# A Trainium2 kernel of two hybrid blocks: scores, pick and dense gates of the expert stage in one stage, and the expert loop's first up sums on another engine

## Chip, cores and metric

The kernel runs on one core of one Trainium2 chip. The metric is device microseconds from start to end of one execution, lower is better. TensorE, VectorE, ScalarE, GpSimd and SyncE are called PE, DVE, ACT, POOL and SP, as in the profile.

## What is computed

Two blocks follow one another on 512 tokens of width 1024. The first is a pool mixer and a gated delta rule, merged, and then an expert layer. The change lies in that layer; the second block (a state-space scan and an attention) is not touched. The expert layer, cut to what matters:

```python
q = (x @ w_query).astype(f32).reshape(b, s, PEER_HEADS, 2, PEER_HALF)       # 8 heads, 2 halves of 128
s1 = jnp.einsum("bshc,hkc->bshk", q[..., 0, :], keys_1.astype(f32))         # 128 keys a half
s2 = jnp.einsum("bshc,hkc->bshk", q[..., 1, :], keys_2.astype(f32))
v1, i1 = lax.top_k(s1, PEER_TOPK)                                           # 16 of 128
v2, i2 = lax.top_k(s2, PEER_TOPK)
cand_score = (v1[..., :, None] + v2[..., None, :]).reshape(...)
cand_idx = (i1[..., :, None] * N_KEYS + i2[..., None, :]).reshape(...)
top_score, pos = lax.top_k(cand_score, PEER_TOPK)                           # 16 of 256 pairs
experts = jnp.take_along_axis(cand_idx, pos, axis=-1)
gates = jax.nn.softmax(top_score, axis=-1)
# for each token, over its 8 x 16 experts e of 16384:
act = gelu(x . expert_down[e])
y += (gate_e * act) * expert_up[e]
```

## The kernel before, in words

Weights are streamed from HBM as tiles of 128 x 1024 fp32 (512 KB), four raw buffers deep. Each tile is split into a high part (ACT, `split_high`, L188) and a low part (DVE or POOL, `split_low`, L197), and a product is three fp32r matmuls of 512 columns (high by high, high by low, low by high), eight chunks to a tile (`mm_columns`, L212 to L214). A tile's split waits until the tile two before it is used up; the next raw load waits for both parts.

The experts are not gathered. The kernel makes a dense gate matrix for all 16384 experts: for each token a 128 x 128 matrix (first key by second key), stored in HBM as `gates`. All expert rows then go through PE: for each first key, a down tile gives 128 experts by 512 tokens, gelu and gate are applied, and an up tile is multiplied.

The stages are functions run one after another by `g.run`, each a block of five engine programs that ends in a barrier of all engines:

- `peer_scores` (L1582): 16 query tiles. PE makes a query tile (24 matmuls) and its scores against the keys (L1618), ACT copies both out, DVE picks 16 of 128 for each of 4 token tiles (`top16`, L1558: MAX8, MATCH_REPLACE8, FIND_INDEX8), POOL splits the weights' low parts and copies values and key numbers to `vals` and `keyno` (L1653).
- `peer_pick` (L1674): PE makes the first 24 down tiles (`EARLY`), ACT applies gelu into `early` (L1736), POOL splits the lows. DVE, for each of four tiles of 128 tokens: 80 candidates (L1780 to L1786), 16 of 80 by `top16`, ranks (L1796 to L1814), then the key numbers by one-hot products over 2048 elements: compare (L1817), multiply (L1822), sum (L1826), each twice; then the softmax's sum (L1829 to L1833), with the exponential on ACT (L1740). PE transposes three rows of 128 (L1751) and DVE copies them into `first`, `second`, `gate` (`keep`, L1772).
- `peer_gates` (L1843): 128 quads of 4 tokens. For each quad DVE makes four one-hot rows of the first key times the gate (L1891) and one of the second key (L1895), POOL two of the second key (L1880), ACT one in two steps (L1919, L1925); PE multiplies them (L1910); ACT copies the result into a staging buffer (L1943) and SP stores a buffer of 8 quads to HBM (L1953). The hot buffers are a ring of four quads. This stage has no down tiles; it is written as loops with register addresses.
- `peer_early` (L1984): loads the gates of 4 first keys at a time (L2005), weighs `early` with them, and multiplies the 24 up tiles.
- `peer_experts` (L2114): a loop of 25 rounds. A round makes 4 down tiles, and the up product of 4 tiles in the Strassen-Winograd form, which needs sums of up tiles. The sums of the first pair (`up_sums`, L2172 to L2177) are made by POOL for the next round, those of the second pair by DVE. ACT rounds the sums up to `up_high` (L2337), DVE makes the low part (L2466). DVE adds the products x = 0 to 6 out of PSUM (L2508).

In `peer_experts` POOL's part, and DVE's order around it, are:

```python
# POOL, L2629 to L2638
first_pair(0)
with steps(pool, 0, LOOPS, 1) as q:
    first_pair(q + 1)
# DVE, end of a round
for x in range(2, 5):
    add(q, x)
low_t43(q + 1, 0)
for x in range(5, 7):
    add(q, x)
```

## Time and profile before

| | |
|---|---|
| median of 3 runs | 3190.7 us (3184.8 to 3194.28) |
| the profiled execution | 3189.76 us, its span 3188.0 us |
| PE busy | 2984.3 us (94%) |
| DVE busy | 2114.2 us (66%) |
| ACT busy | 1287.1 us (40%) |
| POOL busy | 666.3 us (21%) |
| DMA | 312.56 MB, 98 GB/s over the span |
| mean granted clock of PE | 0.971 |

The profile is of one execution. "Busy" is the time in which an engine worked on at least one instruction; PE counts as busy also where it is not at its peak. A view by stretches gives the same by stage, and the timeline gives the start of each instruction, which is where a rate is read: instructions of one engine overlap, so the distance of two starts is what one costs its engine, and its duration is longer. PE is busy 94% of the time, so the first thing to look for is where it is not.

### The profile page before, as it was taken

How to read it: one execution, taken by the hardware profiler on the slowest of the kernel's cores; microseconds unless marked ns; L12 is line 12 of the kernel's file. 1: busy time of each engine (PE TensorE's matmuls, PEld its weight loads, DVE VectorE, ACT ScalarE, POOL GpSimd, SP SyncE). 2: the span in 40 equal slices, each digit the busy share in tenths (PEclk: the TensorE clock that was granted, in tenths of full speed). 3: DMA queues.
4: the chain of work that ended last, by engine and by line, in shares of the span. 5: the costliest groups of instructions: out<-in, count | busy, mean ns of one | idle time of the engine just before them, and what ended most of it. 6: DMA issues, size and time to landing. Idle time of an engine off the chain costs nothing. (4 is left out here: it accounts for less than half of the span.)

```text
span 3188.0 us, 44192 instructions
## 1 busy us (share of the span) xinstructions
PE 2984.3 (94%) x14172; PEld 2414.8 (76%) x14172; DVE 2114.2 (66%) x4082; ACT 1287.1 (40%) x1968; POOL 666.3 (21%) x801
## 2 busy tenths in 40 slices
PE   7999999989897769999999999999998899989997
PEld 5678876867786657788888888888876677866886
DVE  5574435446898968788888888888883683546333
ACT  4443333223336752344444444444444332355222
POOL 1023450003458950111111111111101030024000
PEclk8999999999999989999999999999999899989998
DMA  2210002322223444333334443333432211200321
GB/s 104 79 60 27 28 17 99 107 85 75 78 93 125 184 184 132 125 132 126 125 125 132 132 131 127 125 125 124 131 126 84 75 40 60 93 7 1 126 98 73
DMA packets 137118, 312.56 MB, mean 98 GB/s; under 512 B 9264, under 2 KB 74928, under 8 KB 134832
## 3 DMA queue, kind: packets, MB, share of 16 engines
q1 hardware_dynamic: 136688, 310.74, 28.7%
q8 instruction: 67, 1.10, 0.1%
q10 hardware_dynamic: 320, 0.37, 0.0%
q14 instruction: 43, 0.35, 0.0%
HBM read 273.33 MB, written 37.75 MB: 98 GB/s over the span
## 5 line engine op out<-in xcount | busy, mean ns | idle before, releaser
L188 ACT ACTIVATE split<-raw 128x1024 fp32r<-128x1024 f32 x220 | 231.7, 1059 | 693.3 <-PE merge L214 192.4
L197 DVE TENSOR_TENSOR split<-raw,split 128x1024 fp32r<-128x1024 f32 x172 | 209.7, 1226 | 421.9 <-ACT split L188 421.5
L2109 PE MATMUL up<-up_high,weight_high 128*128 128x512 f32 x700 | 272.3, 389 | 0.0
L2110 PE MATMUL up<-up_low,weight_high 128*128 128x512 f32 x700 | 272.3, 389 | 0.0
L2111 PE MATMUL up<-up_high,weight_low 128*128 128x512 f32 x700 | 272.3, 389 | 0.0
L2172 POOL TENSOR_TENSOR up_sums<-raw 128x512 f32<-128x512 f32 x26 | 33.7, 1296 | 885.8 <-DVE weight_low L2500 885.8
L197 POOL TENSOR_TENSOR split<-raw,split 128x1024 fp32r<-128x1024 f32 x48 | 125.2, 2608 | 365.5 <-ACT split L188 365.5
L1910 PE MATMUL gates<-hot,hot 128*128 128x128 f32 x1024 | 145.4, 289 | 43.8 <-ACT stage L1943 14.5
L1910 PEld LDWEIGHTS gates<-hot,hot 128*128 128x128 f32 x1024 | 125.5, 193 | 63.7 <-DVE hot L1895 43.3
L2238 PE MATMUL dt<-xh,split 128*128 128x512 f32 x416 | 162.2, 390 | 2.7 <-ACTq L2356 1.8
L1880 POOL TENSOR_SCALAR hot<-count,now 128x128 f32<-128x128 f32 x256 | 163.1, 654 | 7.3 <-POOL now L1872 7.3
L1891 DVE TENSOR_SCALAR hot<-count,first,gate 128x128 f32<-128x128 f32 x512 | 155.2, 367 | 12.1 <-PE gates L1910 8.4
L2240 PE MATMUL dt<-xh,split 128*128 128x512 f32 x416 | 161.9, 389 | 0.0
L2239 PE MATMUL dt<-xl,split 128*128 128x512 f32 x416 | 161.9, 389 | 0.0
L2238 PE MATMUL down<-xh,split 128*128 128x512 f32 x416 | 161.8, 389 | 0.0
L2239 PE MATMUL down<-xl,split 128*128 128x512 f32 x416 | 161.8, 389 | 0.0
L2240 PE MATMUL down<-xh,split 128*128 128x512 f32 x416 | 161.8, 389 | 0.0
L2109 PEld LDWEIGHTS up<-up_high,weight_high 128*128 128x128 f32 x700 | 131.4, 188 | 27.4
L2111 PEld LDWEIGHTS up<-up_high,weight_low 128*128 128x128 f32 x700 | 131.4, 188 | 27.3
L2110 PEld LDWEIGHTS up<-up_low,weight_high 128*128 128x128 f32 x700 | 131.4, 188 | 27.2
L212 PE MATMUL proj<-xh,split 128*128 128x512 f32 x352 | 142.0, 403 | 5.2 <-PEq L122 4.5
L2337 ACT ACTIVATE up_high<-up_sums 128x1024 fp32r<-128x1024 f32 x51 | 54.2, 1062 | 222.3 <-POOL up_sums L2177 169.2
(518 smaller groups left out, 7942.0 us busy)
## 6 DMA issues: line engine op xcount, KB each, us to landing
raw<-in_stream SPq DMA_DIRECT2D x440, 512.0 KB, 3.4
gates<-stage SPq DMA_DIRECT2D x16, 2048.0 KB, 6.4
gate<-gates SPq DMA_DIRECT2D x32, 1024.0 KB, 8.2
h<-in_x SPq DMA_DIRECT2D x4, 512.0 KB, 6.0
h<-in_x SPq DMA_DIRECT2D x1, 2048.0 KB, 8.1
rows<-h SPq DMA_DIRECT2D x4, 512.0 KB, 2.6
h<-rows SPq DMA_DIRECT2D x1, 2048.0 KB, 7.8
out<-res SPq DMA_DIRECT2D x8, 256.0 KB, 2.1
```

The costliest lines, as they stand in the source:

```text
L188: act.activation(g.high[t % slots], g.raw[:, t % RAW, :], ACT.Copy).then_inc(g.high_split, 1)
L197: dve.tensor_tensor(g.low[t % slots], g.raw[:, t % RAW, :], g.high[t % slots], ALU.subtract).then_inc(g.low_split, 1)
L212: pe.matmul(out, hi[:, w], xh[:, c, :], start=(c == 0), stop=False)
L1880: ins = pool.tensor_scalar(hot2[:, j, k, :], g.count[:, :], now[:, n:n + 1], None, ALU.is_equal)
L1891: ins = dve.tensor_scalar(hot1[:, j, k, :], g.count[:, :], g.first[:, bass.ds(t, 1)], g.gate[:, bass.ds(t, 1)], ALU.is_equal, ALU.mult)
L1910: ins = pe.matmul(banks[j][:, k * P:k * P + P], hot2[:, j, k, :], hot1[:, j, k, :], start=True, stop=True)
L2109: pe.matmul(bank, wh, uh, start=start, stop=False, skip_group_check=True)
L2110: pe.matmul(bank, wh, ul, start=False, stop=False, skip_group_check=True)
L2111: return pe.matmul(bank, wl, uh, start=False, stop=stop, skip_group_check=True)
L2238: pe.matmul(bank, hi[:, k], g.xh[:, c, :], start=(c == 0), stop=False)
L2239: pe.matmul(bank, hi[:, k], g.xl[:, c, :], start=False, stop=False)
L2240: last = pe.matmul(bank, lo[:, k], g.xh[:, c, :], start=False, stop=(c == DC - 1))
```

## The change

`peer_scores`, `peer_pick` and `peer_gates` become one stage, `peer_route`, with one block. The rows of token tile t (`rows`) are now made on DVE between the instructions of the pick of tile t + 1: one quad of rows after every one to four pick instructions. PE does 5 down tiles after the scores, then for each token tile a `turn`, AT_ONCE down tiles (1, 1, 1, 0), and 32 quads with the chunks of SPREAD (4, 4, 3, 2) down tiles between them, and at last 3 down tiles. The one-hot products of 2048 elements are gone: DVE makes for each rank r a row `chosen` of 256 elements (rank equal to r, times the r-th key number), and PE sums the 16 of them in PSUM while it transposes them (32 fp32r matmuls of 128 columns instead of 2 fp32 transposes). The rows' code is unrolled. ACT issues the stores of the gates. The second staging buffer lies where `h` is, so `h` is written to HBM at the start of the stage and read back at its end; the first gates are loaded at the end of the stage too, and `peer_early` loads each later batch at the end of a step. In `peer_experts` DVE makes the sums of the first pair, after `add(q, 3)`, and POOL does not.

```diff
-def peer_scores(g):
+N_CAND = 80
+QUAD = 4
+GROUP = 32
+QUADS = S // QUAD
+PER_TILE = QUADS // TT
+
+FIRST_DOWN = 5
+AT_ONCE = (1, 1, 1, 0)
+SPREAD = (4, 4, 3, 2)
+
+
+def spread_chunks(t, q):
+
+    n = SPREAD[t] * DC
+    return n * (q + 1) // PER_TILE - n * q // PER_TILE
...
+def peer_route(g):
...
+    stage = [g.at("stage0", R, [P, N_KEYS, GROUP]), g.at("stage1", H_AT, [P, N_KEYS, GROUP])]
...
             @block.sync
             def _(sp):
-                stream_load_each(g, sp, N_QUERY)
+                sp.dma_start(saved, g.h[:, :, :]).then_inc(h_saved, 16)
+                stream_load_each(g, sp, N_QUERY + EARLY)
+                for s in range(2):
+                    sp.wait_ge(stored[s], 16 * S // GROUP // 2)
+
+                sp.dma_start(g.gate[:, :, :, :], g.gates[:, :, 0:4, :].rearrange("n p e t -> p n e t"))\
+                  .then_inc(g.first_gates, 16)
+                sp.dma_start(g.h[:, :, :], saved).then_inc(g.rows_back, 16)
...
+                def turn(t):
+
+                    pe.wait_ge(chosen_made, TOPK * (t + 1) + 1)
+                    pe.wait_ge(step, steps_of * (t + 1))
+                    if t:
+
+                        pe.wait_ge(kept, 3 * t)
+                    for k in range(2):
+                        for r in range(TOPK):
+                            pe.matmul(bank[:, k * P:k * P + P], chosen[:, r, k * hk:k * hk + hk], ident_r[:, :],
+                                      start=(r == 0), stop=(r == TOPK - 1), skip_group_check=True)
+                    pe.transpose(bank[:, 2 * P:3 * P], res[:, :], g.ident[:, :]).then_inc(turned, 1)
...
+                for _ in range(FIRST_DOWN * DC):
+                    down_chunk()
+                for t in range(TT):
+                    turn(t)
+                    for _ in range(AT_ONCE[t] * DC):
+                        down_chunk()
+                    for q in range(PER_TILE):
+                        multiply(t * PER_TILE + q)
+                        for _ in range(spread_chunks(t, q)):
+                            down_chunk()
+                for _ in range((EARLY - n_spread) * DC):
+                    down_chunk()
...
+                        if at == per_group - 1:
+                            act.wait_ge(read, n + 1)
+                            act.dma_start(g.gates[grp], stage[grp % 2][:, :, :]).then_inc(stored[grp % 2], 16)
+                        for j in done_at.get(n - 1, ()):
+                            if q:
+                                down_done(j)
+                        if q == 24 and t + 1 < TT:
+                            grow(t + 1)
...
+                def rows(n):
+                    if n >= 4:
+                        pool.wait_ge(product, n - 3)
...
+                        if q >= 6:
+                            for j in done_at.get(n - 6, ()):
+                                low(j)
+                        rows(n)
...
+                    for h in range(HEADS):
+                        dve.max(best[:, h, 0:8], cand[:, h, :]).then_inc(picked, 1)
+                        if h % 2:
+                            rows(t)
...
-                    for k in range(2):
-                        dve.tensor_tensor(hot[:, k, :, :, :], wide(heads(ranks[:, k, :]), 3),
-                                          g.count[:, 0:TOPK].unsqueeze(1).unsqueeze(1)
-                                          .to_broadcast([P, HEADS, TOPK, TOPK]), ALU.is_equal).then_inc(step, 1)
-                    dve.wait_ge(step, 16 * t + 12)
-                    for k in range(2):
-                        dve.tensor_tensor(hot[:, k, :, :, :], hot[:, k, :, :, :], wide(halves(g.keyno, k), 2),
-                                          ALU.mult).then_inc(hot_made, 1)
-                    for k in range(2):
-                        dve.wait_ge(hot_made, 2 * t + (k + 1))
-                        ins = dve.tensor_reduce(heads(res[:, k, :]), hot[:, k, :, :, :], AX.X, ALU.add)
-                    ins.then_inc(step, 1)
+                    for r in range(TOPK):
+                        dve.scalar_tensor_tensor(
+                            out=chosen[:, r, :].rearrange("p (j k) -> p j k", k=TOPK),
+                            in0=ranks[:, :, :].rearrange("p a (h k) -> p (a h) k", k=TOPK), scalar=float(r),
+                            in1=keyno[:, t, :, r].unsqueeze(2).to_broadcast([P, n_halves, TOPK]),
+                            op0=ALU.is_equal, op1=ALU.mult).then_inc(chosen_made, 1)
+                        if r % 4 == 3:
+                            rows(t)
...
+                for t in range(TT):
+                    pick(t)
+                    while made < t * PER_TILE:
+                        rows(t)
+                    keep(t)
+                while made < QUADS:
+                    rows(TT)
...
@@ def peer_experts, DVE @@
+                first_pair(0)
                 low_t43(0, 0)
...
-                    for x in range(2, 5):
+                    for x in range(2, 4):
                         add(q, x)
+                    first_pair(q + 1)
+                    add(q, 4)
                     low_t43(q + 1, 0)
@@ def peer_experts, POOL @@
-                first_pair(0)
-                with steps(pool, 0, LOOPS, 1) as q:
-                    first_pair(q + 1)
-        g.run(peer_scores)
-        g.run(peer_pick)
-        g.run(peer_gates)
+        g.run(peer_route)
```

Here `done_at` says after which quad a spread down tile is complete (quads 7, 15, 23 and 31 of a token tile with four of them), and `low(j)` is POOL's split of the tile two further on.

Three places show what the order of the instructions has become. The first is DVE in the second half of the pick. Before, from the ranks to the softmax's sum (`hot` is the one-hot product of 2048 elements, `res` its sum):

```order
L1803 CAST partf_7820<-part_7819 128x256
L1806 SCALAR_TENSOR_TENSOR tail_b_7814<-partf_7820 128x128
L1808 TENSOR_SCALAR eight_7815<-partf_7820 128x128
L1809 TENSOR_SCALAR ranks_7813<-partf_7820 128x128
L1811 TENSOR_TENSOR ranks_7813<-ranks_7813,tail_b_7814 128x128
L1812 TENSOR_TENSOR ranks_7813<-partf_7820,tail_b_7814 128x128
L1814 TENSOR_TENSOR ranks_7813<-ranks_7813,eight_7815 128x128
L1817 TENSOR_TENSOR hot_7816<-ranks_7813,count_7810 128x2048 x2
L1822 TENSOR_TENSOR hot_7816<-hot_7816,keyno_6509 128x2048 x2
L1826 TENSOR_REDUCE res_7821<-hot_7816 128x128 x2
L1829 TENSOR_REDUCE total_7822<-res_7821 128x8
```

The same place of a later tile's pick after the change, from the last rank on (`hot` is now a row of a quad of the tile before, `chosen` the selected key numbers of one rank):

```order
L1991 TENSOR_TENSOR ranks_6534<-ranks_6534,eight_6532 128x128
L1918 TENSOR_SCALAR hot_243_6524<-count_6519,first_6516,gate_6517 128x128 x4
L1922 TENSOR_SCALAR hot_242_6523<-count_6519,second_6518 128x128
L1995 SCALAR_TENSOR_TENSOR chosen_6533<-ranks_6534,keyno_6515 128x256 x4
L1918 TENSOR_SCALAR hot_243_6524<-count_6519,first_6516,gate_6517 128x128 x4
L1922 TENSOR_SCALAR hot_242_6523<-count_6519,second_6518 128x128
L1995 SCALAR_TENSOR_TENSOR chosen_6533<-ranks_6534,keyno_6515 128x256 x4
```

Six large instructions have gone, sixteen of 256 elements have come, and a quad of rows (five instructions) stands after every four of them.

The second is POOL in the middle of the new stage, where before it had only splits in one stage and only rows in the other (L1867 is a row, L197 the split of a weight tile):

```order
L1867 TENSOR_SCALAR hot_242_6523<-count_6519,second_6518 128x128 x16
L197 TENSOR_TENSOR split_65<-raw_64,split_65 128x1024
L1867 TENSOR_SCALAR hot_242_6523<-count_6519,second_6518 128x128 x16
L197 TENSOR_TENSOR split_65<-raw_64,split_65 128x1024
L1867 TENSOR_SCALAR hot_242_6523<-count_6519,second_6518 128x128 x6
L197 TENSOR_TENSOR split_65<-raw_64,split_65 128x1024
L1867 TENSOR_SCALAR hot_242_6523<-count_6519,second_6518 128x128 x8
L197 TENSOR_TENSOR split_65<-raw_64,split_65 128x1024
```

Every 8 quads (16 rows) a split now stands between the rows.

The third is DVE near the end of a loop round of `peer_experts` after the change, where before the four lines of `up_sums` stood on POOL alone:

```order
L2571 TENSOR_TENSOR h_61<-h_61,up_340 128x512
...
L2235 TENSOR_TENSOR up_sums_301_12936<-raw_64 128x512
L2236 TENSOR_TENSOR up_sums_302_12937<-raw_64 128x512
...
L2238 TENSOR_TENSOR up_sums_301_12936<-raw_64,up_sums_301_12936 128x512
...
L2240 TENSOR_TENSOR up_sums_302_12937<-up_sums_301_12936,raw_64 128x512
...
L2571 TENSOR_TENSOR acc_12938<-acc_12938,up_340 128x512
...
L2571 TENSOR_TENSOR acc_12938<-acc_12938,up_340 128x512
...
L2529 TENSOR_TENSOR up_low_12935<-up_sums_302_12937,up_high_12934 128x2x512
```

The two additions of product 4 (`acc`) now stand behind the sums, and the low part of the sums (L2529) behind them as before.

## Rows read from the trace of the kernel before

**Rows 1.** The page: PE in 40 slices, and its granted clock

```profile
PE   7999999989897769999999999999998899989997
...
PEclk8999999999999989999999999999999899989998
```

**Rows 2.** Stretches: pick, gates (length; busy PE, PEld, DVE, ACT, POOL; clock)

```profile
838.70:978.80 140.10, 135.40 (x588) 111.23 (x588) 131.13 (x356) 50.59 (x62) 68.06 (x25) 0.98 0.27 91
978.80:1164.90 186.10, 145.38 (x1024) 125.50 (x1024) 172.84 (x640) 139.75 (x392) 170.69 (x288) 0.98 0.40 169
```

**Rows 3.** Timeline (start, length, engine, line): the two handovers, before and after the gates

```profile
973.94 0.49 PE L1751 MATMUL turned<-ident,res 128*128 128x128 f32 x3
...
978.81 1.21 DVE L1891 TENSOR_SCALAR hot<-count,first,gate 128x128 f32<-128x128 f32 x4 [3.66 <-PEq L122]
...
1159.07 4.51 PE L1910 MATMUL gates<-hot,hot 128*128 128x128 f32 x32 [1.08 <-DVE hot L1895]
1159.81 0.32 DVE L1895 TENSOR_SCALAR hot<-count,second 128x128 f32<-128x128 f32 x1
...
1172.12 2.00 ACT L188 ACTIVATE split<-raw 128x1024 fp32r<-128x1024 f32 x2 [7.25 <-PEq L122]
...
1173.28 2.36 DVE L197 TENSOR_TENSOR split<-raw,split 128x1024 fp32r<-128x1024 f32 x2 [13.16 <-ACT split L188]
1179.58 0.69 DVE L2066 TENSOR_TENSOR weight<-early,gate 128x512 f32<-128x512 f32 x1 [3.93 <-DMA gate<-gates]
...
1183.79 0.79 PE L1364 MATMUL up<-split,weight_high 128*128 128x512 f32 x1 [20.22 <-DVE weight_low L2070]
```

**Rows 4.** Timeline of DVE: the first pick

```profile
839.01 0.29 DVE L1780 TENSOR_TENSOR cand<-vals 128x128 f32<-128x128 f32 x1 [1.79 <-POOL count L1720]
...
848.70 2.39 DVE L1803 CAST partf<-part 128x256 f32<-128x256 uint32 x1
...
852.58 6.69 DVE L1817 TENSOR_TENSOR hot<-ranks,count 128x2048 f32<-128x2048 f32 x2
...
870.31 0.27 DVE L1829 TENSOR_REDUCE total<-res 128x8 f32<-128x128 f32 x1
...
871.06 2.49 DVE L1780 TENSOR_TENSOR cand<-vals 128x128 f32<-128x128 f32 x1
```

**Rows 5.** Timeline of POOL: one of its splits beside that pick

```profile
848.55 2.40 POOL L197 TENSOR_TENSOR split<-raw,split 128x1024 fp32r<-128x1024 f32 x1 [9.68 <-ACT split L188]
```

**Rows 6.** Durations by tile: minimum, median, maximum in ns; first and last start

```profile
L1891 DVE TENSOR_SCALAR hot<-count,first,gate x512: 332/341/475, 978.8 to 1159.5; 128x128 f32<-128x128 f32 x171
L1880 POOL TENSOR_SCALAR hot<-count,now x256: 597/652/812, 979.3 to 1161.8; 128x128 f32<-128x128 f32 x128
...
L1817 DVE TENSOR_TENSOR hot<-ranks,count x8: 2291/3387/4482, 852.6 to 954.6; 128x2048 f32<-128x2048 f32 x8
...
L1803 DVE CAST partf<-part x4: 293/294/2387, 848.7 to 950.6; 128x256 f32<-128x256 uint32 x4
```

**Rows 7.** Group of DVE from 838 to 1172: busy us, mean ns; idle before

```profile
L1891 DVE TENSOR_SCALAR hot<-count,first,gate 128x128 f32<-128x128 f32 x512 | 155.2, 367 | 12.1 <-PE gates L1910 8.4 <-PEq L122 3.7
```

**Rows 8.** Timelines: DVE on 256 elements in the loop; PE on 128 columns of fp32r

```profile
1827.31 0.42 DVE L2488 TENSOR_TENSOR weight_sums<-weight 128x256 f32<-128x256 f32 x1
1827.64 0.42 DVE L2489 TENSOR_TENSOR weight_sums<-weight 128x256 f32<-128x256 f32 x1
...
2833.74 0.22 PE L3185 MATMUL logits<-soft_hi,neg_ones_r 128*128 128x128 f32 x1
2833.80 0.27 PE L3185 MATMUL logits<-soft_hi,neg_from_r 128*128 128x128 f32 x1
```

**Rows 9.** Timeline of one loop round's end: who waits for POOL's sums, and DVE

```profile
1815.01 1.06 ACT L2337 ACTIVATE up_high<-up_sums 128x1024 fp32r<-128x1024 f32 x1 [6.68 <-POOL up_sums L2177]
...
1812.19 0.69 DVE L2508 TENSOR_TENSOR acc<-acc,up 128x512 f32<-128x512 f32 x1
```

**Rows 10.** Stretch of the loop: PE, PEld, DVE, ACT, POOL busy us, then clock and DMA

```profile
1400.00:2300.00 900.00, 900.00 (x3972) 745.23 (x3971) 748.13 (x1104) 384.28 (x529) 112.61 (x89) 1.00 0.40 128
```

More of the change, by code:

```diff
@@ new lines, in peer_route @@
+    where = g.at("where", R + 50.75, [P, HEADS, TOPK], U32)
+    part = g.at("part", R + 51, [P, 2, hk], U32)
+    partf = g.at("partf", R + 51.5, [P, 2, hk])
+    tail_b = g.at("tail_b", R + 52.5, [P, hk])
+    eight = g.at("eight", R + 52.75, [P, hk])
+    chosen = g.at("chosen", R + 48, [P, TOPK, 2 * hk], F32R)
+    ranks = g.at("ranks", R + 56, [P, 2, hk])
+    g.gates = nc.dram_tensor("gates", [S // GROUP, P, N_KEYS, GROUP], F32, kind="Internal").ap()
+    saved = nc.dram_tensor("h_saved", [S, D], F32, kind="Internal").ap().rearrange("(t p) d -> p t d", p=P)
@@ new lines, in peer_route @@
+    FIRST, BY_POOL = 3, 2
+    per_half, per_pick, steps_of = 5 * TT, 5 * HEADS, 13
+    done_at, n_spread = tiles_done()
+    (passed, pool_passed, act_passed, q_read, scored, s_read, key_picked, key_kept, counted, summed, picked, step, grown,
+     chosen_made, turned, kept, activated, second_made, first_made, third_made, apart, product, read, h_saved) = (
+        g.sem(x) for x in (
+            "passed", "pool_passed", "act_passed", "query_read", "scored", "score_read", "key_picked", "key_kept",
+            "counted", "summed", "picked", "pick_step", "exp_done", "chosen", "turned", "kept", "activated", "second_hot",
+            "first_hot", "second_hot_by_act", "apart", "product", "read", "h_saved"))
@@ L1601, in peer_scores, with heads @@
+    stored = [g.sem(f"stored{s}") for s in range(2)]
+    per_group = GROUP // QUAD
+    def heads(v):
+        return v.rearrange("p (h k) -> p h k", k=TOPK)
     with ExitStack() as stack:
@@ L1603, in peer_scores @@
         sb = g.banks(stack, 4, "score")
+        down, bank = qb[0:3], qb[3]
         with nc.Block() as block:
@@ L1655, in _ @@
+                for j in range(n_spread, EARLY):
+                    low(j)
             @block.vector
@@ new lines, in _, with rows @@
+                    top16(dve, TT, lambda r: score[:, s, r, :], lambda r: key_work[:, r, :], key_best[:, s, :, :],
+                          key_where[:, s, :, :], key_picked, passed, per_half * j)
+                dve.wait_ge(counted, 1)
+                dve.tensor_copy(ident_r[:, :], g.ident[:, :]).then_inc(chosen_made, 1)
+                dve.wait_ge(key_kept, 2 * N_QUERY)
+                made = 0
+                def rows(upto):
+                    nonlocal made
+                    if made >= upto * PER_TILE:
+                        return
+                    n = made
+                    made += 1
+                    if n >= 4:
+                        dve.wait_ge(product, n - 3)
+                    for k in range(QUAD):
+                        at = n * QUAD + k
+                        ins = dve.tensor_scalar(hot1[:, n % 4, k, :], count[:, :], first[:, at:at + 1],
+                                                gate[:, at:at + 1], ALU.is_equal, ALU.mult)
+                    for k in range(BY_POOL, QUAD - 1):
+                        at = n * QUAD + k
+                        ins = dve.tensor_scalar(hot2[:, n % 4, k, :], count[:, :], second[:, at:at + 1], None,
+                                                ALU.is_equal)
+                    ins.then_inc(first_made, 1)
@@ L1958, in up_free @@
+                for t in range(TT):
+                    pick(t)
+                    while made < t * PER_TILE:
+                        rows(t)
+                    keep(t)
+                while made < QUADS:
+                    rows(TT)
+    g.base += N_QUERY + EARLY
 def up_free(n, n_up, n_banks):
@@ L1973, in four_slots @@
 def four_slots(g):
[L1975 removed]
+    more = g.at("split2", R + 32, [P, 2, 2, TILE], F32R)
     g.high += [more[:, s, 0, :] for s in range(2)]
```

434 lines of the change are left out of this document (195 added, 239 removed).

## The prediction

> **What bounds the kernel now.** I read the page first. PE is busy in nearly every slice but falls to 7 and 6 in the slices from 1036 to 1195 us, and its granted clock to 8 in the last of them [rows 1]. The stretches say which stages those are [rows 2]. In the pick PE is busy 135 of 140 us and DVE 131. In the gates PE is busy 145 of 186, DVE 173, POOL 171. Behind the gates PE stands still for 20.22 us [rows 3]. In the loop's rounds PE is busy 900 of 900 us [rows 10]. So there is time to win between 838 and 1184 us and none inside the loop.
>
> What the two stages need of each engine: 24 down tiles are 24 matmuls each; the loop issues 3972 matmuls in 900 us, 0.227 us each [rows 10], so a tile is 5.44 us and all are 131 us. A quad of gates is 8 matmul records, 32 records in 4.51 us [rows 3], 1.13 us, and 128 of them 144 us. PE could do both in 275 us and takes 345. DVE is what it would then wait for, and so the forecast is a sum over DVE.
>
> **The change, part by part. Rows.** The first row starts at 978.8, the last ends at 1160.1 [rows 3]; DVE idled 12.1 us of these 181.3 [rows 7]. A quad costs DVE 169.2 / 128 = **1.32 us**. The bounds are 1.42 (the whole stage, waits included) and 1.19, if unrolled code and a POOL that is less dense in rows bring the mean of 367 ns down to the minimum of 332 (1.32 x 332 / 367) [rows 6, 7]. I take 1.32, since the instructions are the same.
>
> **Pick.** The first pick runs from 839.01 to the one-hot products at 852.58 [rows 4], 13.6 us, of which its cast stood 2.1 us (2.39 against a minimum of 0.29, rows 6): 11.5 us clean. The one-hot products took until 870.31: 17.7 us, 71 us over four tiles, and they go. In their place are 16 instructions of 256 elements; such starts lie 0.33 us apart [rows 8], so 5.4 us (bound above: 0.42 each, 6.7). The softmax's end, 870.31 to 871.06, stays: 0.75 us. A clean pick is **17.6 us**. The waits between its steps are filled by rows; they are small and I count nothing back.
>
> **Splits of POOL beside rows.** In the trace a POOL split of 2.4 us and a DVE instruction of certain kinds exclude each other: the cast began 0.15 us after the split and ended when it did [rows 4, 5], and a one-hot product took 4.48 us instead of 2.29 [rows 6]. Rows never met a split so far, since the gates' stage has none. Bounds: 0 (a row passes) and 2.4. I take **2.1** per split, since the nearest case in kind is the cast, which like a row reads one SBUF tensor and writes SBUF. Of the splits per token tile (5, 5, 4, 2) one falls into the wait at the tile's end, where DVE reads PSUM: 4, 4, 3, 1 count, 25 us in all.
>
> Here a rule is weighed. While POOL makes rows without pause, DVE's rows take 367 ns in the mean against 332 at least [rows 6, 7]; they do not wait out a POOL row of 652 ns. The Trainium skill, SBUF — State Buffer, section "SBUF: two separate sides", says that a DVE instruction in a two-port mode, or with two SBUF inputs, and a GpSimd instruction that reads SBUF lock each other out for the whole instruction. By that rule of the Trainium skill rows against rows would cost DVE's 1.32 and POOL's 2 x 0.65 one after the other, 2.6 us a quad and 335 us for the gates' stage, and the trace shows 186; the sum would be some 150 us longer by it. I go by the trace. For instructions with two SBUF inputs against POOL's rows nothing in the trace decides, and that is a rival below.
>
> **Turn and keep.** When the last row of a tile is made, PE has a quad to do (1.13), a quad or so of lag (1.3) and a chunk of a down tile (3 x 0.227 = 0.7), then the turn: 32 matmuls of 128 fp32r columns, whose starts are 0.06 apart [rows 8], 1.9 us, and a transpose (bound above: 0.16 each, as the three in 0.49, rows 3, so 5.2). Then DVE's three copies and a wait, 1.1 us. Together **6.3 us** in which DVE makes no row. For the exponential, which ACT now makes between rows, I add 1 us a tile.
>
> **Along DVE.** It starts at 838.0, since of its 1.79 us wait for `count` [rows 4] about 1 goes. Pick 0 has no rows beside it, and 3 of its 5 splits hit: 17.6 + 6.3 = 23.9; PE has its 5 tiles (27 us) meanwhile. Turn and keep without lag: 3.5. Rows begin at 865.4. Tiles 0 and 1: 32 x 1.32 + 17.6 + 8.4 + 1.0 + 6.3 = 75.5 each. Tile 2: 73.4. Tile 3 has no pick: 42.2 + 2.1 = 44.3. The last row is made at 1134.1. PE needs per tile 36 + 27 = 63 us of the 75, so it waits for DVE and not the reverse; ACT and POOL have, per quad, less than in the old stage for a longer time.
>
> **The tail.** After the last quad (1.2) PE has 3 down tiles, 16.3 us: 1151.6. The last handover of this form, PE's turn ending at 974.4 to the first row at 978.8, took 4.4: 1156.0. Then two splits on ACT and DVE, 1172.12 to 1175.64, 3.5 us, and from the first weight to PE's start 4.2 us (1179.58 to 1183.79) [rows 3]: **1163.7**, where before it was 1183.8. Storing the last gates and loading the first hides: before, it lay between the last row's end and 1179.58, 19.5 us; now it is done at 1153.6. If the 3 tiles did not cover it, the tail would be as before. PE's first matmul there lasts 0.79 us [rows 3]; PE now idles 12 us ahead of that start instead of 20, and I count its slow first microseconds the same.
>
> **Moves without cost.** `h` goes out and comes back, 2 MB each. The gates' 3 MB took from 1163.6 to 1179.6, so 11 us bounds each. At the start four raw tiles (21.8 us of PE) cover it; at the end DVE's first addition comes some 4 us after PE starts. Stores now issue from ACT, 16 times: a third of a microsecond each, with ACT busy 140 of 186 us in the old gates and less now.
>
> **The loop.** DVE gets four instructions of 0.69 us at most, 2.8 us a round. It is busy 748 of 900 us [rows 10], 34 of a 40.8 us round, so it fits. In place: ACT waits for the sums until 1815.01; DVE is free for them at 1812.19 [rows 9] and done by 1814.9. The product behind them on DVE (`acc`) is 2.7 us later; its banks are wanted again by PE only after the next round's four down tiles, 21.8 us on. Cost nothing. If that cover were gone, 25 x 2.7 = 67 us. Only in front of the loop PE may start up to 2.5 us sooner, as the sums take half as long; I take 0.
>
> **Sum:** 1163.7 - 1183.8 = -20.1 us, from the profiled 3189.8 to **3169.7**; that execution lies 0.9 below the median of 3190.7. I say 3169.
>
> **The rivals.** A: rows pass a split. The 25 us of stalls go: 3144. For it: rows and rows hardly meet. Against it: the cast. B: the rows keep the pace of the whole old stage, 1.42, because POOL's pair (2 x 0.65) and not DVE set it, and the ring of four quads runs dry when a split comes: 12 us more, 3181. For it: POOL was busy 171 of 186. Against: POOL now has 75 us a tile for 42 + 12 us of work. C: slower. Each of the 25 two-input instructions of a pick waits out a POOL row: 75 of them beside rows x 0.65 = 49 us, 3218. It decides from 0.40 us each. For it: 4.48 against 2.29 was such an instruction against a split. Against: a POOL row holds up a DVE row by 0.03 only. (The Trainium skill's page SBUF — State Buffer has this as its rule.) D: the stage is bound by the chain of turn, keep and exponential, and what is gained in the pick is lost there (some 6 us more at each of three or four turns): no measurable change, 3188.
>
> **How the numbers follow.** What this kernel's measurement can tell from no change is about 0.3%, 9.6 us. Forecast 0.57, A 0.18, B 0.13, C 0.05, D 0.07. Forecast and A are faster, and half of B, which lies on the bound: 0.57 + 0.18 + 0.07 = 0.82. Same: half of B and D less a little, 0.12. Slower: C and a little of D, 0.06. The range reaches from A with its bound of 1.3 a quad (3142) to D with its slack (3192) and leaves out C and the ends.
>
> **What would show it.** Right: the last row of gates near 1134 and PE's next start near 1164; three down tiles behind the last quad; rows in DVE of up to 2.5 us exactly where POOL splits; chosen at 0.33 a start; the loop's PE without idle. Wrong: no row over 0.6 us (A), POOL the one PE waits for (B), chosen instructions near 1 us (C), DVE idle over 10 us at each turn (D), any idle of PE in the loop.

## The result, and the profile after

The changed kernel takes 3173.9 us in the median (3169.6 to 3177.6, 4 runs) against 3189.0 for the kernel before in the same session, a ratio of 0.9949 [0.9935, 0.9963]: 15.1 us faster. The forecast was 3169, 20 us faster, with a range of 3142 to 3192. The profiled execution is the 3169.57 one.

The page of the changed kernel: PE's slices and its clock. The 7, 7 and 6 of PE in [rows 1] are 8, 8 and 8 now, and the clock stays at 9 where it fell to 8.

```profile
PE   7999999988988889999999999999998899989997
...
PEclk8999999999999999999999999999999999989998
```

Stretches of the changed kernel: the first pick, the three phases with a pick among rows, the last tile's rows, and a stretch of the loop (columns as in [rows 2]). DVE is busy 67.97 of 76 us and 66.85 of 75: it is the fullest engine in every phase. In the loop PE is as in [rows 10], DVE has gained 51 us of work and POOL has none.

```profile
838.00:872.00 34.00, 29.12 (x128) 24.98 (x127) 26.11 (x101) 11.47 (x15) 13.51 (x6) 0.87 0.24 78
872.00:948.00 76.00, 66.61 (x415) 58.10 (x414) 67.97 (x261) 45.10 (x112) 55.66 (x70) 0.95 0.35 136
948.00:1023.00 75.00, 65.40 (x410) 56.19 (x409) 66.85 (x260) 44.42 (x110) 56.05 (x70) 0.95 0.38 148
1023.00:1094.00 71.00, 58.92 (x379) 50.40 (x377) 63.61 (x259) 42.85 (x107) 53.50 (x68) 0.95 0.38 145
1094.00:1138.00 44.00, 40.81 (x300) 38.75 (x301) 43.13 (x160) 33.89 (x97) 42.98 (x65) 0.96 0.45 180
...
1400.00:2300.00 900.00, 900.00 (x3972) 745.25 (x3971) 799.30 (x1192) 385.03 (x530) 0.00 (x0) 1.00 0.40 129
```

Timeline of the changed kernel on DVE: the first keep and first rows, a quad that a split of POOL holds up, the end of a tile and the next keep, the last row.

```profile
870.98 0.29 DVE L1930 COPY first<-query 128x128 f32<-128x128 f32 x1 [7.47 <-PE query L1738]
...
872.68 1.26 DVE L1918 TENSOR_SCALAR hot<-count,first,gate 128x128 f32<-128x128 f32 x4
...
877.49 1.10 DVE L1918 TENSOR_SCALAR hot<-count,first,gate 128x128 f32<-128x128 f32 x4
...
878.99 3.26 DVE L1918 TENSOR_SCALAR hot<-count,first,gate 128x128 f32<-128x128 f32 x4
...
938.30 0.28 DVE L1922 TENSOR_SCALAR hot<-count,second 128x128 f32<-128x128 f32 x1
946.47 0.29 DVE L1930 COPY first<-query 128x128 f32<-128x128 f32 x1 [7.90 <-PE query L1738]
...
1136.82 0.32 DVE L1922 TENSOR_SCALAR hot<-count,second 128x128 f32<-128x128 f32 x1
```

And PE where it starts again behind the stage; it was at 1183.79 after 20.22 us idle [rows 3]:

```profile
1167.63 0.79 PE L1367 MATMUL up<-split,weight_high 128*128 128x512 f32 x1 [12.23 <-DVE weight_low L2132]
```

Two measures serve for the kernels below. A **phase** is the time from DVE's first copy of one turned tile to the same copy of the next; the changed kernel has three, of 75.5, 75.1 and 71.5 us, and from the last of these copies to the start of the last row 43.7. The **stage length** runs from the first candidate sum of the first pick to PE's first matmul behind the stage. Single executions differ by some us ahead of that, so absolute times don't compare. It was 1183.79 - 839.01 = 344.8 us before and is 1167.63 - 837.95 = 329.7 now: 15.1 us less, as much as the medians differ. One executed stage against another with the same code shows how far to trust it: in the loop-alone kernel below it was 1184.64 - 843.13 = 341.5, so a difference of 3 us in it means nothing by itself. Medians of different experiments were taken at different times, and the kernel before took 3184.5 to 3190.6 us beside them; so where a kernel below is laid beside the changed kernel, its stage length is given too.

### The profile page after: what moved, and what is told of

Same layout as the page of the kernel before. It is cut to its first block and busy times, and to the rows that moved or that the text cites. A ratio compares the mean times of both kernels' runs of the same rounds, so it can differ in the third digit from the quotient of the medians.

```text
span 3167.9 us, 42380 instructions
## 1 busy us (share of the span) xinstructions
PE 2985.1 (94%) x14292; PEld 2422.8 (76%) x14292; DVE 2139.6 (68%) x4227; ACT 1282.2 (40%) x1960; POOL 526.8 (17%) x664
## 5 line engine op out<-in xcount | busy, mean ns | idle before, releaser
L197 DVE TENSOR_TENSOR split<-raw,split 128x1024 fp32r<-128x1024 f32 x172 | 209.7, 1226 | 435.0 <-ACT split L188 434.6
L365 POOL TENSOR_TENSOR xl<-col,xh 128x512 fp32r<-128x512 f32 x8 | 10.0, 1271 | 1073.1 <-ACT xh L337 1073.1
L1867 POOL TENSOR_SCALAR hot<-count,second 128x128 f32<-128x128 f32 x256 | 172.7, 689 | 36.8 <-PE score L1748 25.7
L1748 PEld LDWEIGHTS score<-hot,hot 128*128 128x128 f32 x1024 | 135.1, 200 | 54.9 <-POOL hot L1867 31.2
L1748 PE MATMUL score<-hot,hot 128*128 128x128 f32 x1024 | 142.9, 288 | 34.3 <-POOL hot L1867 19.1
L1918 DVE TENSOR_SCALAR hot<-count,first,gate 128x128 f32<-128x128 f32 x512 | 172.9, 401 | 0.0
L212 PE MATMUL query<-xh,split 128*128 128x512 f32 x320 | 138.8, 434 | 7.3 <-PEq L122 7.1
```

Source lines behind the costliest of these rows:

```text
L197: dve.tensor_tensor(g.low[t % slots], g.raw[:, t % RAW, :], g.high[t % slots], ALU.subtract).then_inc(g.low_split, 1)
L212: pe.matmul(out, hi[:, w], xh[:, c, :], start=(c == 0), stop=False)
L1748: ins = pe.matmul(sb[n % 4][:, k * P:k * P + P], hot2[:, n % 4, k, :], hot1[:, n % 4, k, :], start=True, stop=True)
L1867: ins = pool.tensor_scalar(hot2[:, n % 4, k, :], count[:, :], second[:, at:at + 1], None, ALU.is_equal)
L1918: ins = dve.tensor_scalar(hot1[:, n % 4, k, :], count[:, :], first[:, at:at + 1], gate[:, at:at + 1], ALU.is_equal, ALU.mult)
```

## Experiments

The edits are given in short form, not line for line.

### Which part of the change gained

**The loop's part undone**: POOL makes the first pair's up sums again.

```
- dve: first_pair(0); in each round, after three additions, first_pair(q + 1)
+ pool: first_pair(0); with steps(pool, 0, LOOPS, 1) as q: first_pair(q + 1)
```

> The changed kernel with its part in the loop undone: GpSimd makes the up sums of each chunk's first pair again (as before the change), VectorE keeps only the additions. Theory: the loop's part was worth nothing, since TensorE is busy 900.00 of the 900 us between 1400 and 2300 in either kernel; so this takes the changed kernel's time, 3174 +- 3, and the only difference is the 1 to 2 us idle of TensorE in front of the loop. Rival: VectorE's up sums (some 51 us of work in that stretch, taken from GpSimd, whose two-input operations had held VectorE up) gave part of the 15 us; then this is slower than the changed kernel by 4 us or more.

3175.1 us, 0.9958 [0.9943, 0.9972], stage length 331.0. Same as the changed kernel. In the stretch of the loop PE is full either way:

```profile
1400.00:2300.00 900.00, 900.00 (x3972) 745.75 (x3971) 746.39 (x1102) 383.98 (x529) 111.97 (x88) 1.00 0.40 129
```

**The loop's part alone**, on the kernel before (the same edit the other way round).

> The kernel before with only the loop's part of the change. Theory: same as before, 3189, within 2.5 us either way, likelier below than above (the two idles of TensorE of 0.8 and 0.9 us on a VectorE split at the start of the loop go). Rival (the loop's part gave some of the 15 us): 3185 or less, TensorE's stretch from the start of the loop to the end shorter by 4 us.

3185.2 us, 0.9990 [0.9975, 1.0004]: not to be told from the kernel before. The loop's part is worth nothing that these runs can show, as forecast.

**The new pick alone**, on the kernel before, its three stages kept.

```
- hot = (rank == count) * key number, 2048 elements, 2 halves; reduce to res
+ for r in range(TOPK): chosen[:, r] = (ranks == r) * keyno[:, t, :, r]
- pe.transpose(bank, res[:, r])                     # r = 0, 1, 2
+ pe.matmul(bank, chosen[:, r, half], ident_r, ...)  # 2 x 16, then one transpose
```

> The kernel before, its three stages kept, with only the new way to pick: the 16 chosen rows and TensorE's 32 short matmuls a token tile in place of the one-hot products and their reductions. Takes about 12 us of VectorE's work a tile (49 in all) out of the pick stage. Theory: TensorE bounds that stage (135.4 busy of 140.5 us, 20.2 of the lead into it apart), and the turns add to it 4 x 3 us: no gain, 3187 to 3197. Rival (the cheaper pick is what gained): 3180 or less, the pick stage 8 us shorter or more.

3200.0 us, 1.0039 [1.0021, 1.0057]: slower, above what I expected. Stretch of its pick, to lay beside the first line of [rows 2]:

```profile
838.31:978.81 140.50, 140.50 (x663) 117.14 (x662) 72.41 (x390) 48.80 (x59) 60.94 (x23) 0.99 0.26 90
```

DVE's 131 us of work have become 72, and nothing came of it, since PE is now busy for all of it. At the pick's end DVE stands for PE:

```profile
984.94 0.29 DVE L1777 COPY first<-turned 128x128 f32<-128x128 f32 x1 [10.43 <-PE turned L1756]
```

The gates' first row starts at 986.74 there, 149.4 us behind the first candidate sum; before it was 978.81 - 839.01 = 139.8. Stage length 351.3 us.

**The overlap undone**: one stage and the new pick stay, but VectorE makes a tile's rows behind its pick.

```
 for t in range(TT):
     pick(t)              # no rows(t) inside any more
     keep(t)
+    while made < (t + 1) * PER_TILE: rows(t + 1)
```

> The changed kernel without its overlap: VectorE picks a token tile with no rows between, and makes that tile's rows behind it; the cheap pick (chosen rows turned by TensorE) and all else stay. Theory (the gain is the overlap): a phase is then a pick of 17.6 us, the exponential, turn and keep of some 6, and 63 us of TensorE's work on chunks and scores, 87 us instead of 75, three times; 36 us slower than the changed kernel, about 3210 (3198 to 3222), so slower than the kernel before, 3187. Rival (the gain is the one-hot products' 12 us of VectorE a tile, and the overlap only moves work): within 8 us of the changed kernel, 3166 to 3182.

3182.6 us, 0.9980 [0.9968, 0.9991], stage length 340.1. My 3210 is refuted: the overlap is worth 9 us, not 36, and the rival's bound of 3182 was just missed too. The phases are 78.1, 78.2 and 76.1 us instead of 75.5, 75.1 and 71.5. Two lines of its timelines show a phase's parts. Rows run from 875.93 to 928.45, where the next pick starts; PE then waits:

```profile
928.45 0.28 DVE L1934 TENSOR_TENSOR cand<-vals 128x128 f32<-128x128 f32 x1
```

```profile
945.97 7.06 PE L1736 MATMUL query<-ident_r,chosen 128*128 128x128 f32 x32 [13.43 <-DVE chosen L1994]
```

The rows with PE's chunks beside them take 52.5 us, 17.5 the pick, 7 the turn. I had put PE's part at 63, from its busy time in the stretches. It isn't that: where PE works on without a gap, a quad and its chunk start 1.585 us apart (in the changed kernel at 936.27, 937.86, 939.44 and 941.03), 50.7 us for 32.

The 7 us are a turn at half the clock. Here is the same turn in the changed kernel, and the stretch of the turn above (granted clock behind the five busy times):

```profile
942.61 3.69 PE L1736 MATMUL query<-ident_r,chosen 128*128 128x128 f32 x32
```

```profile
945.97:953.10 7.13, 7.13 (x34) 7.13 (x35) 0.00 (x0) 0.00 (x0) 0.00 (x0) 0.50 0.01 2
```

Without the overlap PE has nothing to do during a pick: it stood idle 13.4, 13.4 and 14.5 us before its three later turns, and each took 7.06 us at a granted clock of 0.50, where the changed kernel's take 3.69 at 1.00. That is 10.1 us in all, as much as the 10.4 by which the stage grew. VectorE has the same work in either order. So what the overlap saves is, in size, the time that a slow turn costs; a kernel in the serial order whose PE has work before its turns was not tried.

So, in stage lengths: 344.8 before, 351.3 with the cheap pick in its own stage, 340.1 with one stage but no overlap, 329.7 with the overlap. The 59 us that VectorE saves in the pick are worth nothing where PE is the bound. The gain comes with the one stage, in which PE's down chunks lie beside VectorE's rows. How much of it needs the cheap pick isn't shown, since no run has one stage with the old pick; and the third kernel differs from the second in more than the place of the chunks: the quads are written out, two barriers of all engines are gone, and ScalarE stores the gates.

### What a split of POOL beside the rows costs

**Short splits**: 128 of 1024 columns, for the 12 splits that stand among the rows (4, 4, 3 and 1 in the four tiles; seven eighths of their low part is left out). The expectation speaks of 16; the edit leaves the one at each tile's end whole.

```
- pool.tensor_tensor(low[:, :], raw[:, :], high[:, :], subtract)
+ pool.tensor_tensor(low[:, 0:P], raw[:, 0:P], high[:, 0:P], subtract)   # the 12 among rows
```

> The changed kernel, but GpSimd's splits of the first 16 down tiles' low part, which stand among the rows, handle 128 of 1024 columns only (seven eighths of that low part is left out, the rest of the buffer stays as it was). Prices what those splits cost. Theory: each holds a row, a candidate, a part of the sums or the total of VectorE for 1.5 to 2.1 us, and GpSimd's own rows behind it for as long; so the stage ends 16 x 1.5 = 24 us earlier or a little more, 20 to 28 us faster than the changed kernel (3146 to 3154), the phases between two picks' first copies from 75.5, 75.1, 71.5 to about 67 to 69. Rival: the stage is bound by TensorE (66.6 busy of 76 us in the second phase, 65.4 of 75) or by GpSimd's rows, and the splits lie beside that: 0 to 8 us faster.

3149.3 us, 0.9879 [0.9858, 0.9901], 25 us less than the changed kernel; phases 66.6, 66.5, 65.8; stage length 305.7, which is 24.0 less:

```profile
L1865 POOL TENSOR_TENSOR split<-raw,split x12: 456/469/946, 881.8 to 1101.5; 128x128 fp32r<-128x128 f32 x12
```

The expectation's 16 x 1.5 came right by luck. In the changed kernel each of the 12 splits stretched one instruction of VectorE, by 1.65 to 2.17 us over its median and 24.5 in all, so it is 12 x 2.0. The durations by tile (minimum/median/maximum in ns) of the first-key rows, first in the changed kernel, then here:

```profile
L1918 DVE TENSOR_SCALAR hot<-count,first,gate x512: 324/340/2470, 872.7 to 1136.5; 128x128 f32<-128x128 f32 x171
```

```profile
L1925 DVE TENSOR_SCALAR hot<-count,first,gate x512: 319/335/625, 875.6 to 1115.6; 128x128 f32<-128x128 f32 x171
```

The long ones are gone with the long splits. In the changed kernel 10 rows began under a split and took 1993 to 2443 ns; the line at 878.99 above holds one of them, beside this split of POOL:

```profile
878.87 2.38 POOL L197 TENSOR_TENSOR split<-raw,split 128x1024 fp32r<-128x1024 f32 x1 [1.63 <-ACT split L188]
```

**VectorE makes the splits**, the 12 among the rows, the four at the tiles' ends and the three behind the last row:

```
- pool: low(j) before rows(n), at a tile's end, and behind the last row
+ dve:  low(j) at the same places
```

> The changed kernel with the 16 splits among the rows made by VectorE itself (about 1.2 us each, the duration of VectorE's own splits of this size) instead of GpSimd, at the same places in the order of quads. Theory: a split by GpSimd costs VectorE a wait of 1.9 to 2.1 us and GpSimd 2.07, so the exchange of that wait for 1.2 us of work gains 16 x (2.0 - 1.2) = 13 us, 8 to 15 us faster than the changed kernel (3159 to 3166). Rival 1: VectorE is bound by its own work and the waits lie mostly in its idle time: slower by up to 16 x 1.2 = 19 us. Rival 2 (TensorE bounds the stage): no change.

3160.4 us, 0.9913 [0.9891, 0.9935]: 13.5 us less than the changed kernel, where the first theory had 8 to 15, although the busiest engine was given more to do; stage length 315.2, 14.5 less. The group's line from the first row to the last, 1214 ns each:

```profile
L197 DVE TENSOR_TENSOR split<-raw,split 128x1024 fp32r<-128x1024 f32 x15 | 18.2, 1214 | 13.0 <-ACT split L188 13.0
```

The theory's sum came right, its terms didn't. From the first row to the last it is 251.1 us instead of 264.5, 13.4 less. Instead of 24.5 us of being held up VectorE has 18.2 of its own splits, 6.3 less. The other 7 are idle time: VectorE idles 16.4 us in that stretch, 23.6 in the changed kernel.

### What the handover costs

**Early turns**: PE turns tiles 1 to 3 in front of the last four quads of the tile before.

```
 for q in range(PER_TILE):
+    if q == PER_TILE - 4 and t + 1 < TT: turn(t + 1)
     multiply(...)
```

> The changed kernel with TensorE's turns of tiles 1 to 3 put in front of the last four quads of the tile before, instead of behind them (nothing else moves). In the changed kernel VectorE ends its rows of a tile at 938.30 and gets the turned tile at 946.47, because TensorE still has 3 or 4 quads, their down chunks and the turn of 3.5 us to do. Theory (those handovers, 8 us each, are on the path): the turn ends about 6 us earlier in each of three tiles, phases of about 69, 69 and 66 instead of 75.5, 75.1 and 71.5, so 3156 (3153 to 3163), 18 us faster than the changed kernel. Rival (TensorE, busy 66.6 of 76 us, or GpSimd with its splits fills the time): 0 to 5 us faster, and the idle time of VectorE moves from the handover into the rows.

3177.5 us, 0.9957 [0.9940, 0.9974], stage length 331.1: no gain, the theory missed. Phases 69.0, 74.0 and 71.0, and the last tile took 52.9 us, not 43.7: with an early turn four quads are still to be multiplied when the turned tile is copied, so a phase by itself doesn't show a gain. Waits of the stage, first in the changed kernel, then here (us in total, times, longest):

```profile
POOL split L197 <- ACT split L188: 28.6, 13, 7.3
...
DVE first L1930 <- PE query L1738: 23.2, 3, 8.0
```

```profile
POOL split L197 <- ACT split L188: 39.4, 13, 11.0
...
DVE hot L1921 <- PE score L1748: 18.6, 6, 6.7
DVE first L1933 <- PE query L1738: 11.5, 4, 7.5
```

With the first keep the changed kernel's VectorE idles 23.2 + 7.5, some 30.7 us, for PE; here it is 18.6 + 11.5 = 30.1. The wait has gone from the handover into the rows.

**Early turns with VectorE's splits**:

> Both: the 16 splits among the rows by VectorE, and the turns of tiles 1 to 3 in front of the last four quads. Theory: the two take different waits away; VectorE is then busy 64.2 us of a phase that was 69.8, TensorE 63.7, so phases of 65 to 66 and 4 us less in each of three: 3148 (3144 to 3153). Rival (they compete for the same idle time, or ACT's high parts hold VectorE's splits, 4.3 us at each tile's end): 3156 to 3160, no better than the splits alone.

3165.6 us, 0.9921 [0.9904, 0.9937]: 5 us above the splits alone, with intervals that overlap, but the stage length, 322.7 against 315.2, says the same. VectorE now stood at the tile's last split, which needs ScalarE's high part, which needs the down tile that PE ends with the tile's last quad:

```profile
946.09 1.23 DVE L197 TENSOR_TENSOR split<-raw,split 128x1024 fp32r<-128x1024 f32 x1 [7.50 <-ACT split L188]
```

**The last split of a tile behind two quads of the next tile**, with early turns; once with POOL's splits, once with VectorE's:

```
+ if q == 2 and t: last_lows(t - 1)      # in the next tile
- last_lows(t)                           # at the tile's end
```

> Turns of tiles 1 to 3 in front of the last four quads, and GpSimd's last split of a tile (which waits for ScalarE's high part, which waits for the down tile that TensorE ends with the tile's last quad) moved from the tile's end behind the first two quads of the next tile. With the turns alone GpSimd stood 10.85 and 10.07 us at that split at the tiles' ends and made no row of the next tile. Theory (that split is what took the handover's place): phases of about 69, 69 and 67, the last tile 44 to 47 us, 14 us less than the changed kernel, 3160 (3156 to 3167). Rival (TensorE or VectorE fills the phase anyway): 3172 to 3178, as with the turns alone.

3168.9 us, 0.9946 [0.9928, 0.9963]; phases 71.0, 75.2, 70.7, last tile 52.1, stage length 332.7: no gain again, so this split was not what took the handover's place. The waits:

```profile
DVE hot L1926 <- PE score L1748: 16.5, 4, 6.5
DVE first L1938 <- PE query L1738: 14.7, 4, 7.5
```

31.2 us together, again what it was. My reading: there are four buffers for rows, so VectorE waits for a product before its fifth quad ahead in any case, and PE is behind by those quads and a down tile wherever the turn stands. The sums of waits fit it; a deeper ring wasn't tried.

> The same with VectorE making the 16 splits: its last one of a tile behind two quads of the next tile. With splits and early turns together VectorE stood 7.5 us at that split before it took the turned tile, and the kernel was slower than with the splits alone. Theory: VectorE busy 64 us a phase and no long wait, so phases of 65 to 66 and 44 for the last tile: 3148 (3142 to 3154). Rival (TensorE's lag is the bound): 3158 to 3166.

3154.7 us, 0.9903 [0.9886, 0.9919], above the 3148 of the theory and within neither range: stage length 312.9, against 315.2 with the splits alone. Repaired, the early turn is worth no more than this measure can tell.

### A faster version, and the first turn

**Even load**: three edits on the last kernel.

```
+ three second-key rows by POOL in odd quads of tiles 0 to 2 (VectorE makes none there)
+ act: distance and last_row of the next tile's first 4 quads, then down_done of the last tile
- if q >= 6: low(done_at[n - 6]);  + if q >= 7: low(done_at[n - 7])
```

> The last kernel (VectorE's splits, early turns, last split behind the next tile's first quads) with three more things, each for a wait that its trace shows: GpSimd makes three of the second-key rows, not two, in every other quad of tiles 0 to 2 (VectorE 68 busy of 69, GpSimd 47); ScalarE makes the next tile's first four third rows before it ends the last down tile (TensorE waited 5.1 us for one in the last tile); each split one quad later (VectorE waited 22 us in 9 places for ScalarE's high part). Theory: TensorE's own pace bounds what is left, a quad and its down chunk at 1.585 us: 32 of them, 8 more chunks of 1.12 and a turn of 3.7 are 63.4 us a phase, so phases of 64 to 65, 65 and 60, 10 us less than the last kernel: 3144 (3137 to 3151). Rival (GpSimd, now 57 busy, with VectorE's rows slowed by it, bounds): 3152 to 3160.

3147.5 us, 0.9862 [0.9834, 0.9890], 38 us under the kernel before in the medians; phases 61.2, 66.7, 65.4, the last tile 49.1, stage length 305.1. The time is the theory's, but its working had an error: a chunk is 3 x 0.227 = 0.68 us of PE, not 1.12, so PE's own pace is 50.7 + 5.4 + 3.7 = 59.8 us a phase, and the phases lie above it. In the first stretch below VectorE is again full, 64.66 of 65 us. Which of the three edits gained was not tried.

```profile
875.00:940.00 65.00, 60.16 (x397) 53.04 (x397) 64.66 (x263) 40.66 (x105) 59.94 (x85) 0.99 0.34 131
940.00:1005.00 65.00, 59.62 (x399) 52.68 (x398) 60.49 (x242) 43.71 (x109) 54.17 (x79) 1.00 0.42 171
```

**A down tile in front of the first turn** instead of behind it, on the even-load kernel.

```
- for _ in range(FIRST_DOWN * DC): down_chunk()
+ for _ in range((FIRST_DOWN + AT_ONCE[0]) * DC): down_chunk()
```

> The last kernel with one down tile (8 chunks, 24 matmuls at 0.227 us) moved from behind the first turn to in front of it. In the changed kernel TensorE ends its five down tiles, stands idle 4.9 us for the first pick (5.2 here) and makes the first turn at a granted clock of 0.50: 7.1 us for 32 matmuls, where the three later turns take 3.4 to 3.7. The tile takes 5.4 us and so fills that gap. Theory (the idle time lowers the clock, the low clock doubles the turn, and the first rows wait for it): the first turn takes 3.4 to 3.7 us, the first copies of the turned tile come 3 us earlier against the first candidate (33.1 us behind it now, 30 then), and TensorE has 6.9 us less behind it; 3 to 6 us faster, 3143 (3138 to 3148). Rival (the first turn is slow for another reason, its operands or the bank): the turn stays 6.6 to 7 us, the copies come no earlier, and the time stays 3147 +- 2.

The first turn without and with it:

```profile
867.18 7.06 PE L1740 MATMUL query<-ident_r,chosen 128*128 128x128 f32 x32 [4.87 <-DVE res L2021]
```

```profile
867.78 3.69 PE L1740 MATMUL query<-ident_r,chosen 128*128 128x128 f32 x32
```

The granted clock over the turn (the value behind the five busy times), in the changed kernel and here:

```profile
863.60:871.00 7.40, 7.35 (x34) 7.38 (x35) 0.02 (x1) 0.00 (x0) 0.00 (x0) 0.50 0.21 71
```

```profile
867.50:871.20 3.70, 3.70 (x34) 3.62 (x33) 0.00 (x0) 0.00 (x0) 0.00 (x0) 1.00 0.39 142
```

Behind some 4.9 us in which PE did nothing it is at 1.2 GHz, with work in that gap at 2.4. The slow stretch has not gone altogether: behind the turn PE now stands idle 3.4 us for the first rows, and from 873.3 to 880.1 it is granted 0.50. The turned tile's first copy comes 30.0 us behind the first candidate sum instead of 33.1, as expected, and the stage length is 301.0 instead of 305.1 (1142.66 - 841.66 against 1146.57 - 841.49). In whole times it is 3144.7 us, 0.9873 [0.9851, 0.9895]: not to be told from the 0.9862 of even load.

## Why the prediction was right, point by point

The number missed by 5 us, and 4.0 of these can be placed: the stage length was forecast as 1163.7 - 838.0 = 325.7 and measured 329.7. That is the sum of three errors, +7.3, -4.2 and +0.9 us, and it is luck that the second takes back more than half of the first; without it the time would have come out 9 us above the forecast, near 3178, still inside the range.

- **Start of rows: missed by 7.3 us.** Forecast 865.4 - 838.0 = 27.4 us behind the first candidate sum, measured 872.68 - 837.95 = 34.7. The mis-sized term is the turn. "32 matmuls of 128 fp32r columns, whose starts are 0.06 apart, 1.9 us" took two matmuls of [rows 8] as the pace of 32. The later turns run at 0.11 us each (942.61 to 946.02, 3.4 us), nearer to my upper bound of 0.16. The first ran at half the clock, 7.1 us, which is 5.2 of the 7.3 us: I had counted on PE being done in time and not asked at what clock it would go on after waiting. Another 1.7 are the pick's, which ended at 863.50, 25.6 us from its start and not 23.9: four of its splits held it up, by 8.1 us in all, where three by 2.1 were forecast. One of the four fell on its last multiplication.
- **From the first row to the last: 4.2 us too long.** Forecast 268.7, measured 264.5. The phases came out at 75.5, 75.1 and 71.5 against 75.5, 75.5 and 73.4. That is partly luck: the handover, 6.3 us forecast, is 8.6 (last row's end at 938.58, next candidates at 947.19), most of the difference being the turn, 3.7 instead of 1.9; and what lies between two handovers is 66.9 us, not 69.2. The exponential's 1.0 costs nothing, since rows go on around it; the remaining 1.3 I can't place.
- **Splits beside rows: right in kind and size.** Forecast 12 splits of 2.1 us, 25 in all; the trace has 24.5, and the short splits took 24.0 off the stage. It was eleven first-key rows and a chosen instruction that a split held up (one of the rows began 0.01 us ahead of it), and in the first pick a candidate sum, a part, a chosen instruction and the last multiplication. Rival A (rows pass a split) is out. The row that decided for it was the cast under a split [rows 4, 5, 6].
- **Pick, no cover elsewhere: right for VectorE; what it does to POOL was not foreseen.** A clean pick was forecast at 17.6 us; with the overlap undone it takes 17.5 (928.45 to 945.97). The 16 chosen instructions took 409 ns at least and 414 in the median, and the 27 that began under a row of POOL no more than 508. Rival C needed 1.0 us each there. It was POOL that waited: its row takes 0.62 us in the median, and of the 15 rows that overlap chosen instructions five took 1.11 to 2.07. In the changed kernel, two rows of POOL and the four chosen instructions beside them:

```profile
925.65 2.83 POOL L1867 TENSOR_SCALAR hot<-count,second 128x128 f32<-128x128 f32 x2 [1.51 <-PE score L1748]
...
926.65 1.43 DVE L1995 SCALAR_TENSOR_TENSOR chosen<-ranks,keyno 128x256 fp32r<-128x256 f32 x4
```

  The second of these rows began at 926.42 and took 2.07 us. The Trainium skill, SBUF — State Buffer, section "SBUF: two separate sides", says that of a VectorE instruction with two SBUF inputs and a GpSimd one that reads SBUF the first to start has the shared port for its whole length, and the other blocks. For POOL's splits of 1024 columns this kernel agrees (two chosen instructions lasted 2.58 and 2.62 us there). For its rows of 128 the exclusion shows too, but not the order: the row at 926.42 was the first to start, and it was the one that was stretched.
- **Rival B** (POOL sets the pace): not in the form given, since VectorE is busy 68 of 76 us and POOL 56. But POOL's rows are what PE's matmuls wait for most in the stage, 19.1 us in 14 places, 13.7 of them behind a split.
- **Rival D** (the handover eats it): no, but its size was underrated. The first keep's 7.5 and the three later ones' 23.2 us are idle time of VectorE, and moving the turn did not give them back.
- **Tail: 0.9 us off.** Forecast 29.6 from the last row to PE's start, measured 1167.63 - 1137.14 = 30.5. The three down tiles covered the storing and loading of gates; PE idled 12.2 us.
- **Loop: right.** Zero, by two experiments from two sides.

The expectations made later were worse than the prediction where they priced a wait by its length (early turns) and PE's need by its busy time (no overlap).

## What to carry to other kernels

Before you move work off an engine, ask which engine ends last in that stretch: 59 us less of VectorE's work made this kernel slower while the stage was TensorE's. Before you call an overlap's gain the time that it hides, look at the clock: in the serial order TensorE stood idle and then took 7.06 us for a turn of 3.69, and three such turns are as long as all that the overlap saved. A wait that looks idle in a ring of buffers is often the other side's lag: move the thing waited for and the wait reappears a few buffers on, so sum the waits of both places before and after. And where two engines lock each other out for a long instruction, try to give that instruction to the engine that would wait for it: here 1.2 us of work was cheaper than 2 us of waiting.

## What the runs showed that I had not expected

- A first-key row of VectorE (one tensor input, two scalars per partition, 128 elements, 0.34 us in the median) that begins under a split of POOL lasts until that split ends, up to 2.47 us; under POOL's own rows it takes 341 ns in the median, with POOL idle 339.
- The exclusion works both ways. A split of POOL that was due at 860.06, among chosen instructions of VectorE 0.33 us apart, took 3.29 us instead of 2.4, while they went on at 0.41 each; VectorE's multiplication behind them, begun at 861.62, then took 1.88 instead of 0.29. POOL's short rows are stretched by chosen instructions as well, from 0.62 to 2.07 us at most.
- Matmuls of 128 columns in fp32r start 0.11 us apart at a granted clock of 1.00, and 0.22 at 0.50, where the two I had read were 0.06 apart.
- TensorE stood 4.88 us behind full work and was then granted 0.50 for the next 7.4 us of short matmuls; with 5.4 us of work put into that gap it kept 1.00 through the turn. One tile of work moved ahead of a turn halved the turn. With the overlap undone all four turns come behind idle time, 4.9 to 14.5 us, and all four are granted 0.50.
